# Who makes and who scales the one-hot rows when gates are spread: all eight rows in one VectorE instruction, three scaled by GpSimd

## The chip, the cores and the metric

The kernel runs on one core of one Trainium2 chip. The metric is the device time of one execution in microseconds. The compute engines of the core are TensorE (PE in the profile), VectorE (DVE), ScalarE (ACT) and GpSimd (POOL); SyncE (SP) issues transfers.

## The reference

The kernel computes one step of a small hybrid decoder: a Mamba-2 group and an RWKV-7 group, and then a mixer over 16,384 single-neuron experts ("PEER"). Only the last part bears on the change. Each token picks, for each of 8 heads, 16 experts out of 128 x 128. An expert is named by two keys, and each pick has a gate:

```python
e1 = jnp.take_along_axis(i1, pos // PEER_TOPK, axis=-1)
e2 = jnp.take_along_axis(i2, pos % PEER_TOPK, axis=-1)
experts = e1 * N_KEYS + e2
gate = jax.nn.softmax(top_s, axis=-1)
...
act = jax.nn.gelu(jnp.einsum('thkd,td->thk', ue, tb).astype(F32), approximate=False) * gate
```

So a token has 8 x 16 = 128 picks (first key, second key, gate). For 704 of the tokens the kernel doesn't gather the picked experts. It runs every expert on every token and multiplies by a dense table of gates, 128 x 128 numbers per token, which is zero where nothing was picked.

## The kernel before

The program is a row of stages: input projection, the two groups' heads, output projection, the picking of experts, the turning of some rows, `spread_gates`, and at last `run_experts`, which takes about half of the time. Each stage ends in a barrier of all engines.

`spread_gates` builds the dense table of gates. The 704 tokens are 11 groups of 64 (`GROUP_ROWS`), each group is 8 batches of 8 tokens (`BATCH`), so there are 88 batches. First TensorE turns the picks so that a token's 128 picks lie on the 128 partitions (`by_pick`: first key, second key, gate). Then, for a token t, with one partition per pick:

- `hot_i[:, t, :]` is a row of 128 numbers per pick: 1 at the first key and 0 elsewhere. VectorE makes it by comparing `iota` (0 to 127) with the key.
- `gate_j[:, t, :]` is the same for the second key, times the gate.
- TensorE multiplies the one by the other, over the picks: the result in PSUM is the token's 128 x 128 table.
- ScalarE copies eight such tables from PSUM into `spread`, and after eight batches SyncE stores that to memory.

Who makes `gate_j` is divided: for the first five tokens (`SCALED = 5`) VectorE makes only the ones, in one instruction, and ScalarE multiplies each by its gates in place (`scale`, line 2259, five instructions). For the other three VectorE makes and multiplies in one `tensor_scalar` per token (line 2302). GpSimd has no work in this stage.

`hot_i`, `gate_j`, the PSUM tables `g_ps` and `spread` have two buffers each. Batches use them in turn. Every engine runs its own program over the batches, and counting semaphores hold it: VectorE may begin batch i when the matmuls of batch i-2 are done (`g_done`); ScalarE scales when the five rows are there (`hot_ready`), and it does this for batch i+1 before it empties batch i; TensorE needs VectorE's last instruction of the batch (`batch_ready`), ScalarE's scales (`scaled`) and the emptied PSUM tables of batch i-2 (`g_out`).

Of the kernel before, what the change touches and what calls it, by code (L numbers as in the profile page):

```python
# [22 lines left out]
ALU = mybir.AluOpType  # L23
# [3 lines left out]
P = 128  # L27
# [25 lines left out]
START = 2  # L53


class Stage:
# [15 lines left out]
    def sb(self, name, shape, dt=F32):  # L72
        return self.ctx.enter_context(self.nc.sbuf_tensor(f"{self.name}_{name}", shape, dt))

    def psum(self, name, *shape):

        n = int(np.prod(shape))
        banks = self.ctx.enter_context(self.nc.psum_tensor(f"{self.name}_{name}", [P, -(-n // BANK) * BANK], F32))
        used = banks[:, 0:n]
        return used if len(shape) == 1 else used.rearrange("p (a b) -> p a b", a=shape[0])  # L80

    def sem(self, name):
        self.sems.append(self.nc.alloc_semaphore(f"{self.name}_{name}"))
        return self.sems[-1]
# [13 lines left out]
def at(dram, m):  # L98

    return dram[m] if isinstance(m, int) else dram[bass.ds(m, 1)].rearrange("a p c -> (a p) c")  # L100
# [1656 lines left out]
N_KEYS = 128  # L1757
# [417 lines left out]
BATCH = 8  # L2175

SCALED = 5


def spread_gates(nc, picks, gates_d, eye_d, iota_d):  # L2180
    with Stage(nc, "spread") as st:
        sb, psum, sem = st.sb, st.psum, st.sem
        eye, iota = sb("eye", [P, P]), sb("iota", [P, P])

        by_pick = sb("by_pick", [P, 3, ROW_GROUPS * GROUP_ROWS])
        hot_i = [sb(f"hot_i_{s}", [P, BATCH, N_KEYS]) for s in range(2)]
        gate_j = [sb(f"gate_j_{s}", [P, BATCH, N_KEYS]) for s in range(2)]
        spread = [sb(f"spread_{s}", [P, N_KEYS, GROUP_ROWS]) for s in range(2)]
        g_ps = [psum(f"g_ps_{s}", BATCH, P) for s in range(2)]
        t_ps = [psum(f"t_ps_{s}", BANK) for s in range(2)]  # L2190
        consts_loaded, turned, turned_out = sem("consts_loaded"), sem("turned"), sem("turned_out")
        batch_ready, hot_ready, scaled, g_done, g_out = sem("batch_ready"), sem("hot_ready"), sem("scaled"), sem("g_done"), sem("g_out")
        stored = [sem(f"g_stored_{s}") for s in range(2)]
        PER_GROUP = GROUP_ROWS // BATCH

        def over_groups(eng, before, batch, after):

            def group(q, s, g):
                before(q, s, g)
                with eng.Fori(0, PER_GROUP // 2) as b:  # L2200
                    for a in range(2):
                        batch(s, a, g * PER_GROUP + b * 2 + a, b * 2 + a)
                after(q, s, g)

            with eng.Fori(0, ROW_GROUPS // 2) as q:
                for s in range(2):
                    group(q, s, q * 2 + s)
            group(ROW_GROUPS // 2, 0, ROW_GROUPS - 1)

        nothing = lambda *_: None  # L2210
        with nc.Block() as block:
            @block.sync
            def _(sp):
                sp.dma_start(eye[:], eye_d).then_inc(consts_loaded, 16)
                sp.dma_start(iota[:], iota_d).then_inc(consts_loaded, 16)

                def store(q, s, g):
                    sp.wait_ge(g_out, START + g * PER_GROUP + PER_GROUP)
                    sp.dma_start(at(gates_d, g), spread[s][:].rearrange("p j t -> p (j t)")).then_inc(stored[s], 16)

                over_groups(sp, nothing, lambda *_: None, store)
                for s in range(2):
                    sp.wait_ge(stored[s], START + 16 * ((ROW_GROUPS + 1 - s) // 2))

            @block.tensor
            def _(pe):
                pe.wait_ge(consts_loaded, START + 32)
                for a, tile in enumerate(DENSE_TILES):
                    n = ROW_TILES[tile][1]
                    if a >= 2:  # L2230
                        pe.wait_ge(turned_out, START + a - 1)
                    for s in range(3):
                        mm = pe.transpose(t_ps[a % 2][:, s * P:s * P + n], picks[0:n, s, tile, :], eye[0:n, 0:n])
                    mm.then_inc(turned, 1)

                def batch(s, a, i, b):
                    pe.wait_ge(batch_ready, START + i + 1)
                    pe.wait_ge(scaled, START + i + 1)

                    pe.wait_ge(g_out, START + i - 1)  # L2240
                    for t in range(BATCH):
                        mm = pe.matmul(g_ps[a][:, t, :], hot_i[a][:, t, :], gate_j[a][:, t, :], start=True, stop=True)
                    mm.then_inc(g_done, 1)

                over_groups(pe, nothing, batch, nothing)

            @block.scalar
            def _(act):
                for a, tile in enumerate(DENSE_TILES):
                    lo, n = ROW_TILES[tile]  # L2250
                    act.wait_ge(turned, START + a + 1)
                    by_slice = t_ps[a % 2][:, 0:3 * P].rearrange("p (s t) -> p s t", s=3)[:, :, 0:n]
                    act.activation(by_pick[:, :, lo:lo + n], by_slice, ACT.Copy).then_inc(turned_out, 1)

                def scale(i, a):
                    act.wait_ge(hot_ready, START + i + 1)
                    for t in range(SCALED):
                        gate = by_pick[:, 2, bass.ds(i * BATCH + t, 1)]
                        last = act.activation(gate_j[a][:, t, :], gate_j[a][:, t, :], ACT.Copy, scale=gate)
                    last.then_inc(scaled, 1)  # L2260

                def empty(s, a, i, b):
                    act.wait_ge(g_done, START + i + 1)
                    act.activation(spread[s][:, :, bass.ds(b * BATCH, BATCH)], g_ps[a].rearrange("p t j -> p j t"), ACT.Copy).then_inc(g_out, 1)

                def group(q, s, g, pairs):
                    act.wait_ge(stored[s], START + q * 16)
                    with act.Fori(0, pairs) as b:
                        for a in range(2):
                            i = g * PER_GROUP + b * 2 + a  # L2270
                            scale(i + 1, 1 - a)
                            empty(s, a, i, b * 2 + a)


                scale(0, 0)
                with act.Fori(0, ROW_GROUPS // 2) as q:
                    for s in range(2):
                        group(q, s, q * 2 + s, PER_GROUP // 2)
                group(ROW_GROUPS // 2, 0, ROW_GROUPS - 1, PER_GROUP // 2 - 1)
                last_batch = ROW_GROUPS * PER_GROUP - 1  # L2280
                scale(last_batch, 1)
                empty(0, 0, last_batch - 1, PER_GROUP - 2)
                empty(0, 1, last_batch, PER_GROUP - 1)

            @block.vector
            def _(dve):
                dve.wait_ge(consts_loaded, START + 32)
                dve.wait_ge(turned_out, START + len(DENSE_TILES))

                def batch(s, a, i, b):  # L2290

                    dve.wait_ge(g_done, START + i - 1)
                    def hot(out, key, rows):
                        cube = [P, rows, N_KEYS]
                        return dve.tensor_tensor(out, iota[:].unsqueeze(1).broadcast_to(cube),
                                                 by_pick[:, key, bass.ds(i * BATCH, rows)].unsqueeze(2).broadcast_to(cube), ALU.is_equal)

                    hot(gate_j[a][:, 0:SCALED, :], 1, SCALED).then_inc(hot_ready, 1)
                    last = hot(hot_i[a][:], 0, BATCH)
                    for t in range(SCALED, BATCH):  # L2300
                        e2, gate = (by_pick[:, s_, bass.ds(i * BATCH + t, 1)] for s_ in (1, 2))
                        last = dve.tensor_scalar(gate_j[a][:, t, :], iota[:], e2, gate, ALU.is_equal, ALU.mult)
                    last.then_inc(batch_ready, 1)

                over_groups(dve, nothing, batch, nothing)

            @block.gpsimd
            def _(pool):
                st.start(pool)


class RowTiles:
# [664 lines left out]
```

## Time and profile before

| | |
|---|---|
| median of three runs | 4279.36 us (4277.87 to 4286.69) |
| the profiled execution: its time, its span | 4278.28 us, 4276.7 us |
| TensorE busy, share of the span | 3743.9 us, 88% |
| VectorE | 3242.4 us, 76% |
| ScalarE | 1204.4 us, 28% |
| GpSimd | 1241.3 us, 29% |
| `spread_gates`, first batch's start to last batch's copy | 1984 to 2221 us |

The shares are means over stages that differ; for a change inside one stage only that stage's rows count. In a row of the timeline or of the groups stand the line of the kernel, the engine, the operation, what it writes and reads by the program's names, and the shape as partitions x elements of one instruction. A matmul in fp32 leaves two records. An instruction's record on VectorE or ScalarE can overlap the next one's by some hundredths of a microsecond, so the pace is read from start to start.

### The profile page before, as it was taken

The numbers are of one execution on the slowest core, as the hardware profiler recorded it, in microseconds if no ns is written. First come the engines' busy times: TensorE is split into PE (matmuls) and PEld (weight loads), VectorE is DVE, ScalarE is ACT, GpSimd is POOL, SyncE is SP. The second block draws the span as 40 slices with busy tenths as digits, with TensorE's granted clock in tenths as the row PEclk, the third lists the DMA queues.
The fourth block names the chain that finished last, engine by engine and source line by source line (L and its number), as shares of the span: only waits on it lengthen the run. The fifth ranks groups of instructions, "written<-read, shape, count | busy, mean of one in ns | idle before, by whom it ended". The sixth has DMA issues, their size and how long they took to land. (4 is left out here: it accounts for less than half of the span.)

```text
span 4276.7 us, 66020 instructions
## 1 busy us (share of the span) xinstructions
PE 3743.9 (88%) x22546; PEld 3450.8 (81%) x22546; DVE 3242.4 (76%) x6415; ACT 1204.4 (28%) x2213; POOL 1241.3 (29%) x1054
## 2 busy tenths in 40 slices
PE   7998666999895868774769999999999999999997
PEld 6998554777785845443759999999999999999997
DVE  4431564666764248997977999999999999999998
ACT  3211232232322102215972222222222222222221
POOL 0211000000000000000004555556555555555563
PEclk8999566899998889887989999999999999999998
DMA  3775211000001100010458888888888888888885
GB/s 93 85 80 75 82 59 62 24 12 20 11 9 62 67 23 27 29 39 42 201 228 299 291 293 300 292 300 287 300 289 299 289 300 291 298 294 287 305 289 190
DMA packets 292099, 729.43 MB, mean 171 GB/s; under 512 B 27528, under 2 KB 138840, under 8 KB 290448
## 3 DMA queue, kind: packets, MB, share of 16 engines
q0 software_dynamic: 120560, 431.42, 32.6%
q1 hardware_dynamic: 171424, 296.57, 20.7%
q8 instruction: 60, 0.98, 0.1%
q14 instruction: 55, 0.45, 0.0%
HBM read 650.20 MB, written 77.70 MB: 170 GB/s over the span
## 5 line engine op out<-in xcount | busy, mean ns | idle before, releaser
L2512 POOL DMA_INDIRECT experts_u_row<-in_up_rows,experts_u_at x384 | 562.5, 1465 | 648.1 <-DVE experts_dot L2698 530.2
L107 PE MATMUL experts_up_ps<-experts_u_hi,experts_up_hi 128*128 128x352 f32 x2048 | 662.4, 323 | 26.8 <-DVE experts_u_lo L2674 24.7
L107 PE MATMUL experts_down_ps<-experts_act_hi,experts_down_hi 128*128 128x352 f32 x2048 | 675.4, 330 | 8.2 <-DVE experts_down_lo L2674 6.4
L108 PE MATMUL experts_down_ps<-experts_act_lo,experts_down_hi 128*128 128x352 f32 x2048 | 661.6, 323 | 0.0
L108 PE MATMUL experts_up_ps<-experts_u_lo,experts_up_hi 128*128 128x352 f32 x2048 | 661.2, 323 | 0.0
L109 PE MATMUL experts_up_ps<-experts_u_hi,experts_up_lo 128*128 128x352 f32 x2048 | 661.0, 323 | 0.0
L109 PE MATMUL experts_down_ps<-experts_act_hi,experts_down_lo 128*128 128x352 f32 x2048 | 660.9, 323 | 0.0
L2519 POOL DMA_INDIRECT experts_v_row<-in_down,experts_v_at x384 | 506.3, 1318 | 222.4 <-issue 112.8
L2698 DVE CUSTOM_DVE_ANT_0 experts_u_row<-experts_u_row,stream_u_rows_of 128x1024 f32<-128x1024 f32 x384 | 466.5, 1215 | 71.8 <-DMA experts_u_row<-in_up_rows,experts_u_at 68.8
L2711 DVE SCALAR_TENSOR_TENSOR stream_h_rows_of<-experts_v_row,experts_weight,stream_h_rows_of 128x1024 f32<-128x1024 f32 x384 | 496.0, 1292 | 14.2 <-DVE experts_weight L2703 6.8
L2717 DVE TENSOR_TENSOR stream_h<-stream_h,experts_down_ps 128x704 f32<-128x704 f32 x512 | 450.4, 880 | 68.0 <-PE experts_down_ps L109 67.1
L107 PEld LDWEIGHTS experts_down_ps<-experts_act_hi,experts_down_hi 128*128 128x128 f32 x2048 | 385.8, 188 | 31.4 <-DVE stream_h L2717 19.8
L107 PEld LDWEIGHTS experts_up_ps<-experts_u_hi,experts_up_hi 128*128 128x128 f32 x2048 | 386.2, 189 | 29.3 <-issue 21.7
L108 PEld LDWEIGHTS experts_down_ps<-experts_act_lo,experts_down_hi 128*128 128x128 f32 x2048 | 386.8, 189 | 0.0
L108 PEld LDWEIGHTS experts_up_ps<-experts_u_lo,experts_up_hi 128*128 128x128 f32 x2048 | 386.7, 189 | 0.0
L109 PEld LDWEIGHTS experts_up_ps<-experts_u_hi,experts_up_lo 128*128 128x128 f32 x2048 | 386.6, 189 | 0.0
L109 PEld LDWEIGHTS experts_down_ps<-experts_act_hi,experts_down_lo 128*128 128x128 f32 x2048 | 386.1, 189 | 0.0
L2616 ACT ACTIVATE experts_down_hi<-experts_down 128x1024 fp32r<-128x1024 f32 x128 | 135.4, 1057 | 707.6 <-PE experts_down_ps L109 707.6
L1984 PE MATMUL pick_q_ps<-picking_u,pick_w_query 128*128 128x384 f32 (+1 forms) x768 | 249.3, 485 | 44.0 <-DMA pick_sub_keys<-in_keys 44.0
L2629 ACT ACTIVATE experts_act_v<-experts_up_ps 128x352 f32<-128x352 f32 x256 | 119.0, 465 | 596.2 <-PE experts_up_ps L109 454.0
L107 PE MATMUL inp_proj<-inp_u_hi,inp_w_in_hi 128*128 128x384 f32 x648 | 222.5, 343 | 45.0 <-DVE inp_u_lo L290 23.0
L1984 PEld LDWEIGHTS pick_q_ps<-picking_u,pick_w_query 128*128 128x128 f32 x768 | 149.1, 197 | 134.7 <-issue 56.5
(380 smaller groups left out, 6626.5 us busy)
## 6 DMA issues: line engine op xcount, KB each, us to landing
experts_up<-in_up SPq DMA_DIRECT2D x128, 512.0 KB
experts_down<-in_down SPq DMA_DIRECT2D x128, 512.0 KB
gates<-spread_spread SPq DMA_DIRECT2D x11, 4096.0 KB
experts_gates<-gates SPq DMA_DIRECT2D x64, 704.0 KB
cols<-inp_done POOLq DMA_DIRECT2D x27, 576.0 KB
inp_w_in<-in_w_in SPq DMA_DIRECT2D x27, 512.0 KB
pick_w_query<-in_w_query SPq DMA_DIRECT2D x16, 512.0 KB, 4.0
experts_u_row<-in_up_rows,experts_u_at POOLq DMA_INDIRECT x384
```

The lines of the kernel that those rows point to most:

```text
L107: pe.matmul(out, w_hi, x_hi, start=start, stop=False)
L108: pe.matmul(out, w_hi, x_lo, start=False, stop=False)
L109: return pe.matmul(out, w_lo, x_hi, start=False, stop=stop)
L1984: mm = pe.matmul(q_ps[at_q % 3][:, 0:n], w[s][:, k * P:k * P + P], u[:, k, lo:lo + n], start=(k == 0), stop=(k == KD - 1))
L2512: pool.indirect_dma_start(u_row[b][:], None, up_rows_d, bass.IndirectOffsetOnAxis(ap=u_at[slot][:, b, a:a + 1], axis=0)).then_inc(u_row_lo ...
L2519: pool.indirect_dma_start(v_row[b][:], None, v_table, bass.IndirectOffsetOnAxis(ap=v_at[slot][:, b, a:a + 1], axis=0)).then_inc(v_row_load ...
L2616: act.activation(down_hi[:, e, :], down[e][:], ACT.Copy).then_inc(down_rounded, 1)
L2629: act.activation(act_v[e][:, lo:lo + n], up_ps[e][c][:, 0:n], ACT.Gelu).then_inc(gelu_ready, 1)
L2698: dve.tensor_tensor_reduce(u_row[b][:], u_row[b][:], rows.u[:, b, :], 1.0, 0.0, ALU.mult, ALU.add, dot[slot][:, b, a:a + 1]).then_inc(dott ...
L2711: dve.scalar_tensor_tensor(out=rows.h[:, b, :], in0=v_row[b][:], scalar=weight[slot][:, b, a:a + 1], in1=rows.h[:, b, :], op0=ALU.mult, op ...
L2717: dve.tensor_tensor(row, row, down_ps[m % 2][:, :, 0:DC], ALU.add).then_inc(added, 1)
```

## The change

VectorE now makes the ones of all eight second keys in one instruction, and then `hot_i`. The three `tensor_scalar` are gone. ScalarE scales rows 0 to 4 as before. GpSimd multiplies rows 5 to 7 by their gates in place, in one `tensor_tensor` per batch, when `hot_ready` is raised, and raises a new semaphore, `pool_scaled`, for which TensorE waits as well.

```diff
@@ TensorE
                     pe.wait_ge(batch_ready, START + i + 1)
                     pe.wait_ge(scaled, START + i + 1)
+                    pe.wait_ge(pool_scaled, START + i + 1)
@@ VectorE
-                    hot(gate_j[a][:, 0:SCALED, :], 1, SCALED).then_inc(hot_ready, 1)
-                    last = hot(hot_i[a][:], 0, BATCH)
-                    for t in range(SCALED, BATCH):
-                        e2, gate = (by_pick[:, s_, bass.ds(i * BATCH + t, 1)] for s_ in (1, 2))
-                        last = dve.tensor_scalar(gate_j[a][:, t, :], iota[:], e2, gate, ALU.is_equal, ALU.mult)
-                    last.then_inc(batch_ready, 1)
+                    hot(gate_j[a][:], 1, BATCH).then_inc(hot_ready, 1)
+                    hot(hot_i[a][:], 0, BATCH).then_inc(batch_ready, 1)
@@ GpSimd
+                def batch(s, a, i, b):
+                    pool.wait_ge(hot_ready, START + i + 1)
+                    rows = BATCH - SCALED
+                    cube = [P, rows, N_KEYS]
+                    pool.tensor_tensor(gate_j[a][:, SCALED:BATCH, :], gate_j[a][:, SCALED:BATCH, :],
+                                       by_pick[:, 2, bass.ds(i * BATCH + SCALED, rows)].unsqueeze(2).broadcast_to(cube), ALU.mult).then_inc(pool_scaled, 1)
+
+                over_groups(pool, nothing, batch, nothing)
```

On VectorE, inside the loop over the batches of a group, one batch read as follows before:

```order
-L2295 ISA
-L2295 TENSOR_TENSOR spread_gate_j<-spread_iota,spread_by_pick 128x640
-L2295 ISA
-L2295 TENSOR_TENSOR spread_hot_i<-spread_iota,spread_by_pick 128x1024
-L2302 ISA
-L2302 TENSOR_SCALAR spread_gate_j<-spread_iota,spread_by_pick 128x128
-L2302 ISA
-L2302 TENSOR_SCALAR spread_gate_j<-spread_iota,spread_by_pick 128x128
-L2302 ISA
-L2302 TENSOR_SCALAR spread_gate_j<-spread_iota,spread_by_pick 128x128
```

and two batches in a row read as follows after the change:

```order
+L2296 ISA
+L2296 TENSOR_TENSOR spread_gate_j<-spread_iota,spread_by_pick 128x1024
+L2296 ISA
+L2296 TENSOR_TENSOR spread_hot_i<-spread_iota,spread_by_pick 128x1024
+L2293 REGISTER_ALU
+L2296 ISA
+L2296 TENSOR_TENSOR spread_gate_j<-spread_iota,spread_by_pick 128x1024
+L2296 ISA
+L2296 TENSOR_TENSOR spread_hot_i<-spread_iota,spread_by_pick 128x1024
```

The instruction for `gate_j` grew from five rows to eight, and `hot_i` is now the last of a batch. On GpSimd, whose program went straight from the barrier ahead of the stage to the one behind it, the loop over the batches is new:

```order
+L2312 TENSOR_TENSOR spread_gate_j<-spread_gate_j,spread_by_pick 128x384
+L2309 REGISTER_ALU
+L2312 ISA
+L2312 TENSOR_TENSOR spread_gate_j<-spread_gate_j,spread_by_pick 128x384
+L2200 REGISTER_ALU
+L2200 COMPARE_AND_BRANCH
```

It has one multiply of 3 x 128 elements per partition in each batch. The programs of TensorE (but for its third wait), ScalarE and SyncE are what they were.

## Rows read from the trace of the kernel before

**Rows 1.** Windows, gate spreading: busy us of PE, PEld, DVE, ACT, POOL; granted clock; DMA, GB/s
```profile
2010.00:2220.00 210.00, 163.15 (x1279) 148.50 (x1278) 208.10 (x395) 196.07 (x475) 0.00 (x0) 1.00 0.47 200
```

**Rows 2.** Groups of the stage: busy us, mean ns | idle before, releaser
```profile
L2242 PE MATMUL spread_g_ps<-spread_gate_j,spread_hot_i 128*128 128x128 f32 x1408 | 181.8, 283 | 55.4 <-DVE spread_gate_j L2302 55.4
...
L2259 ACT ACTIVATE spread_gate_j<-spread_gate_j,spread_by_pick 128x128 f32<-128x128 f32 x440 | 138.2, 389 | 16.4 <-DVE spread_gate_j L2295 16.3
...
L2302 DVE TENSOR_SCALAR spread_gate_j<-spread_iota,spread_by_pick 128x128 f32<-128x128 f32 x264 | 74.3, 332 | 0.0
L2295 DVE TENSOR_TENSOR spread_gate_j<-spread_iota,spread_by_pick 128x640 f32<-128x640 f32 x88 | 71.2, 809 | 19.5 <-ACT spread_by_pick L2253 18.1 <-PE spread_g_ps L2242 1.4
```

**Rows 3.** Timeline in mid-stage: start, duration (us), engine, line, operation
```profile
2091.32 0.81 DVE L2295 TENSOR_TENSOR spread_gate_j<-spread_iota,spread_by_pick 128x640 f32<-128x640 f32 x1
...
2091.52 2.05 PE L2242 MATMUL spread_g_ps<-spread_gate_j,spread_hot_i 128*128 128x128 f32 x16 [0.59 <-DVE spread_gate_j L2302]
2092.05 1.21 DVE L2295 TENSOR_TENSOR spread_hot_i<-spread_iota,spread_by_pick 128x1024 f32<-128x1024 f32 x1
2092.28 1.57 ACT L2259 ACTIVATE spread_gate_j<-spread_gate_j,spread_by_pick 128x128 f32<-128x128 f32 x5 [0.16 <-DVE spread_gate_j L2295]
2093.19 0.85 DVE L2302 TENSOR_SCALAR spread_gate_j<-spread_iota,spread_by_pick 128x128 f32<-128x128 f32 x3
2093.76 1.01 ACT L2264 ACTIVATE spread_spread<-spread_g_ps 128x1024 f32 x1
2093.96 0.81 DVE L2295 TENSOR_TENSOR spread_gate_j<-spread_iota,spread_by_pick 128x640 f32<-128x640 f32 x1
...
2094.17 0.82 PE L2242 MATMUL spread_g_ps<-spread_gate_j,spread_hot_i 128*128 128x128 f32 x5 [0.60 <-DVE spread_gate_j L2302]
```

**Rows 4.** All first instructions of a batch (ns); timeline of the stage's two ends
```profile
L2295 DVE TENSOR_TENSOR spread_gate_j<-spread_iota,spread_by_pick x88: 804/808/826, 1984.2 to 2215.4; 128x640 f32<-128x640 f32 x88
...
1987.06 5.12 PE L2242 MATMUL spread_g_ps<-spread_gate_j,spread_hot_i 128*128 128x128 f32 x26 [3.93 <-DVE spread_gate_j L2302]
...
1990.97 1.02 ACT L2264 ACTIVATE spread_spread<-spread_g_ps 128x1024 f32 x1 [1.57 <-PE spread_g_ps L2242]
1991.00 0.82 DVE L2295 TENSOR_TENSOR spread_gate_j<-spread_iota,spread_by_pick 128x640 f32<-128x640 f32 x1 [1.44 <-PE spread_g_ps L2242]
...
2218.23 2.05 PE L2242 MATMUL spread_g_ps<-spread_gate_j,spread_hot_i 128*128 128x128 f32 x16 [0.59 <-DVE spread_gate_j L2302]
2220.32 1.02 ACT L2264 ACTIVATE spread_spread<-spread_g_ps 128x1024 f32<-128x1024 f32 x1 [1.61 <-PE spread_g_ps L2242]
```

**Rows 5.** Experts' stage, GpSimd's timeline: two copies beside two-input instructions of VectorE
```profile
2290.47 0.83 POOL L2500 COPY experts_u_at<-stream_expert_at 128x6 uint32<-128x6 uint32 x1
...
2307.09 0.37 POOL L2504 COPY experts_v_at<-stream_expert_at 128x6 uint32 x1
```

**Rows 6.** VectorE's timeline at those two copies
```profile
2290.37 0.89 DVE L2689 TENSOR_TENSOR experts_act_v<-experts_act_v,experts_gates 128x704 f32<-128x704 f32 x1
...
2306.20 1.21 DVE L2698 CUSTOM_DVE_ANT_0 experts_u_row<-experts_u_row,stream_u_rows_of 128x1024 f32<-128x1024 f32 x1
2307.34 0.08 DVE L2698 DVE_READ_ACCUMULATOR2_ANT experts_dot<- 128x1 f32 x1
2307.34 1.27 DVE L2711 SCALAR_TENSOR_TENSOR stream_h_rows_of<-experts_v_row,experts_weight,stream_h_rows_of 128x1024 f32<-128x1024 f32 x1
```

**Rows 7.** All copies of the two lines: ns min/median/max, first and last start
```profile
L2500 POOL COPY experts_u_at<-stream_expert_at x64: 197/807/1272, 2234.9 to 4175.7; 128x6 uint32 x60, 128x6 uint32<-128x6 uint32 x4
...
L2504 POOL COPY experts_v_at<-stream_expert_at x64: 193/369/432, 2276.9 to 4226.2; 128x6 uint32 x60, 128x6 uint32<-128x6 uint32 x4
```

**Rows 8.** GpSimd's memsets, groups by shape: busy us, mean ns
```profile
L1067 POOL MEMSET rwkv_s_seq<- 128x1024 f32 x1 | 1.0, 952 | 5.0 <-POOLq L70 5.0
...
L1068 POOL MEMSET rwkv_start_rows<- 128x128 f32 x1 | 0.2, 205 | 0.0
```

**Rows 9.** A window in an earlier stage, columns as in rows 1
```profile
990.00:1000.00 10.00, 6.91 (x56) 5.89 (x56) 9.96 (x20) 1.86 (x6) 0.00 (x0) 1.00 0.51 194
```

More of the change, by code:

```diff
@@ L2191, in spread_gates @@
         consts_loaded, turned, turned_out = sem("consts_loaded"), sem("turned"), sem("turned_out")
-        batch_ready, hot_ready, scaled, g_done, g_out = sem("batch_ready"), sem("hot_ready"), sem("scaled"), sem("g_done"), sem("g_out")
+        batch_ready, pool_scaled, hot_ready, scaled, g_done, g_out = sem("batch_ready"), sem("pool_scaled"), sem("hot_ready"), sem("scaled"), sem("g_done"), sem("g_out")
         stored = [sem(f"g_stored_{s}") for s in range(2)]
```

## The prediction

> **What bounds the kernel now.** I read the windows of the whole stage first. While the gates are spread, TensorE is busy 163 of 210 us, ScalarE 196, VectorE 208, and GpSimd not at all; the clock granted to TensorE is 1.00, its 2.4 GHz [rows 1]. So VectorE is the candidate, and the groups of the stage say the same: its instructions have next to no idle time before them once the stage runs, while the matmuls idle 55.4 us, all of it waiting for VectorE's `tensor_scalar` of line 2302 [rows 2]. Then one batch of eight tokens in the timeline [rows 3]. VectorE's first instruction of a batch starts at 2091.32 and the next batch's at 2093.96 us: the period is 2.64 us. It is made of three start-to-start steps with no gap between them: 0.73 us for the five one-hot rows of `gate_j`, 1.14 us for the eight of `hot_i` (the record says 1.21, but the next instruction starts 0.07 before its end), and 0.77 us for the three `tensor_scalar`. The others have room: ScalarE needs 1.48 + 1.00 = 2.48 us of the 2.64 and waits 0.16, TensorE needs 2.05 and waits 0.59. The first start is at 1984.2 and the last at 2215.4 [rows 4], 87 steps in 231.2 us, or 2.66 each: 87 times 2.64 is 229.7, and the missing 1.5 us are the first two batches, in which TensorE still ran at 1.2 GHz (first batch from 1987.06 to about 1990.97, 3.91 us instead of 2.05) [rows 4].
>
> The stage ends in a barrier and the next one starts behind it, so what a period gains or loses is multiplied by 88 and reaches the end undiminished. The profiled execution took 4278.28 us (span 4276.7), 1.1 us under the median of the three runs, 4279.36; the sum is made against 4278.3. About 0.2%, 8.6 us or 0.10 us per period, is what a measurement of this kernel can tell from no change.
>
> **The change part by part.** *VectorE.* Five rows become eight: the same instruction as `hot_i`'s, which the trace has at 1.14 us from start to start, in place of 0.73: +0.41. The three `tensor_scalar` go: -0.77. VectorE's own work falls from 2.64 to 2.28 us per batch. Alone, that would be 88 x 0.36 = 32 us.
>
> *The loop through two buffers.* It does not come to that, for `gate_j` of batch i+2 may only be written when the matmuls of batch i are done. Counted from the start of `gate_j` in batch i: 1.21 us to its end (five rows before: 0.81), 0.15 until ScalarE starts (2092.13 to 2092.28), 1.57 for its five scales, 0.13 until TensorE starts (as from 2094.04, VectorE's end, to 2094.17) [rows 3], 2.09 until another engine sees the batch done (2218.23 to 2220.32) and 0.03 more for VectorE (1991.00 against ScalarE's 1990.97) [rows 4]. Sum 5.18 us for two batches, 2.59 each. ScalarE's own floor is 2.48. So with a GpSimd that costs nothing the period would be 2.59 and the gain 88 x 0.05 = 4 us. The longer first instruction delays ScalarE by 0.41 us, and that eats what VectorE saves.
>
> *GpSimd's multiply.* It may start when `gate_j` is whole, 1.36 us behind its start, as ScalarE does. At that moment VectorE is already 0.22 us into `hot_i`, which has two inputs in SBUF. What happens then, the stage of before cannot show, but the experts' stage can. There GpSimd copies six words per partition, 64 times from each of two lines; the shortest copies take 0.197 and 0.193 us, the medians are 0.807 and 0.369 [rows 7]. Beside a two-input instruction of VectorE a copy takes what is left of that one: started at 2290.47 beside a plain `TENSOR_TENSOR` that ends at 2291.26, it ended at 2291.30; started at 2307.09 beside one that ends at 2307.41, at 2307.46 [rows 5, 6]. So a GpSimd instruction that reads SBUF stands still for as long as VectorE reads two tensors. The Trainium skill has this as a rule, in "SBUF — State Buffer", section "Who interferes with whom": VectorE's second input and GpSimd's read use one interface, held as an exclusive lock for a whole instruction. By that rule the two engines' times add in each batch; without it the period would be 2.59. The trace agrees where GpSimd comes second.
>
> The second copy also says who is next. VectorE had a two-input instruction ready directly behind (it starts at 2307.34, 1.27 us long), and the copy still ended at 2307.46, not at 2308.6. The waiting GpSimd instruction gets in at the boundary. That VectorE in its turn stands still for as long as GpSimd reads, no row shows (six words are over at once). I take it, since the standstill seen is complete and would be odd if it went one way only; the other answer is a rival below.
>
> So a batch becomes: `gate_j` 1.14, `hot_i` 1.14, then GpSimd's multiply while VectorE waits with the next `gate_j`. How long is a multiply of 3 x 128 elements? The trace has none. Nearest are GpSimd's memsets, 0.205 us for 128 words per partition and 0.952 for 1024 [rows 8]: 0.83 ns a word and 0.10 fixed. A multiply that ran at a memset's pace would take 0.42 us, the lower bound. One that moves its three words per element (two read, one written) one after the other: 3 x 0.32 + 0.10 = 1.06, and with 0.15 for handing over, 1.2 as the upper bound. I take two reads one after the other with the write beside them, 0.74, and 0.16 for handing over (what ScalarE needs behind VectorE): 0.90. A GpSimd that read both tensors at once is not excluded, so both ends stay in the range. The Trainium skill ("GPSIMD Engine Reference", section "Elementwise — side-by-side cycle accounting") measured 4497 ns for 2048 elements of a two-input add. Scaled to 384 that is an estimate of 0.84 us, and with it the period would be some 0.04 to 0.1 us from mine.
>
> Period 2.28 + 0.90 = 3.18 us. Nothing else is later: GpSimd ends at about 3.2, TensorE starts at 3.3 and is done at 5.4, and `gate_j` two batches on is due at 6.36; ScalarE's 2.48 and TensorE's 2.05 fit. VectorE's permit for the next `gate_j` comes at 5.4 - 3.18 = 2.2, just before `hot_i` ends, so it does ask at the boundary. Loss 3.18 - 2.64 = 0.54 us, x 87 = 47. The start is 0.5 us cheaper (the cold first batch is partly hidden), and the last batch 0.56 longer from `gate_j` to matmul: they cancel. The stores of `spread` would start every 25 instead of 21 us (eight batches), and ScalarE, which must wait for an earlier one, idles for VectorE and TensorE alone [rows 2]. GpSimd had nothing else to do here, and its next work is behind the barrier. **4278.3 + 47 = 4325 us.** With the bounds 0.42 and 1.2: GpSimd is then done at 2.8 and ScalarE's 2.93 decides when TensorE may start, but VectorE's 2.70 still sets the period: +5 us; and 3.48, +74 us. The likeliest case by itself: 4283 to 4352.
>
> **The rivals.** *GpSimd runs beside VectorE for nothing* (not slower). Period 2.59, 4274 us, inside 0.2%. It holds if the multiply, started at 1.36, is done by ScalarE's 2.93, so up to 1.57 us long; above 1.67 us it turns into a loss. For it: only six-word copies of integers show the standstill. Against: they show it each time, plain `TENSOR_TENSOR` included. 0.11. If some of my latencies of a tenth also shrink and ScalarE's 2.48 becomes the period, 88 x 0.16 = 14 us are gained, 4264: 0.04.
>
> *VectorE wins the boundary.* It then runs four instructions, 4.56 us, until it needs the first batch's matmuls; GpSimd goes 4.56 to 5.46, TensorE from 5.59, done for VectorE at 7.71. Period 3.86, +1.22 x 88 = 107, 4385 us. For it: in the row that speaks against it a one-column accumulator read (0.08 us) lies between the two instructions and may have been the gap; here there is none. 0.08.
>
> *VectorE is not held*, only GpSimd: its multiply then ends at 3.18, TensorE's batch is done for VectorE 0.13 + 2.12 later, and half of 5.43 is 2.72 per batch: +0.08 x 88 = 7, 4285 us; up to 4297 (2.85) where each slows the other somewhat. 0.08.
>
> *TensorE's clock falls.* It would be busy 2.05 of 3.18 us, 64%, with a pause of 1.1 us per batch. The trace has 1.00 beside 69% [rows 9], little above that. At 1.2 GHz a batch takes 3.91 [rows 4], and that would be the period: +1.27 x 88 = 112, 4390 us. 0.04.
>
> **How the numbers follow.** The case of 4325 has 0.65. Range 4284 to 4392: from a VectorE that is not held up to the low clock. It leaves out the cases of 4274 and 4264 and about 0.04 at its edges: 0.2 in all. Slower: 0.65 + 0.08 + 0.04, and 0.05 of the 0.08 of a VectorE not held: 0.82. Within 0.2%: 0.11 + 0.03 = 0.14. Faster: 0.04.
>
> **What would show it.** In the profile after: VectorE's `gate_j` starts about 3.18 us apart; each GpSimd multiply ends shortly behind the end of a `hot_i`, plus its own 0.8; the first instruction of a batch shows either a gap before it or more than its 1.21 us, while `hot_i` keeps 1.21; TensorE waits for GpSimd, about 1.1 us per batch, its clock 1.00; ScalarE's wait grows from 0.16 to 0.7. Starts every 2.6 us with multiplies that lie wholly inside `hot_i` would prove the lock wrong; two `gate_j` in a row, then a gap, that VectorE wins; a multiply of 1.5 us or more, that my price was off.

## The result and the profile after

The changed kernel takes 4315.47 us (median of four runs, 4311.34 to 4321.48) against 4280.38 us before in the same comparison (four runs): a ratio of 1.0081, 95% interval 1.0063 to 1.0098. It is slower by some 35 us. The profiled execution has a span of 4314.0 us. A second, later comparison (4282.72 us, six runs, against 4264.27, 17 runs) gave 1.0059 (1.0036 to 1.0082); what is known of the difference is told below.

The tile view of `gate_j` after the change gives, for each kind of instruction, its shortest, median and longest duration in ns, and the first and last start. It answers to [rows 4].

```profile
L2296 DVE TENSOR_TENSOR spread_gate_j<-spread_iota,spread_by_pick x88: 1225/1540/1850, 1997.6 to 2251.1; 128x1024 f32<-128x1024 f32 x88
L2312 POOL TENSOR_TENSOR spread_gate_j<-spread_gate_j,spread_by_pick x88: 1528/1621/1637, 1999.1 to 2252.9; 128x384 f32<-128x384 f32 x88
```

From the first to the last `gate_j` it is now 253.5 us, before 231.2: the stage lost 22.3 us, 0.26 us per batch. VectorE's comparison of 1024 elements takes 1.54 us for `gate_j`, although the same comparison for `hot_i` still takes 1.21, and GpSimd's multiply is recorded with 1.62 us. The timeline of mid-stage answers to [rows 3].

```profile
2090.41 1.62 POOL L2312 TENSOR_TENSOR spread_gate_j<-spread_gate_j,spread_by_pick 128x384 f32<-128x384 f32 x1 [1.28 <-DVE spread_gate_j L2296]
...
2091.57 1.54 DVE L2296 TENSOR_TENSOR spread_gate_j<-spread_iota,spread_by_pick 128x1024 f32<-128x1024 f32 x1 [0.23 <-PE spread_g_ps L2243]
...
2092.27 2.05 PE L2243 MATMUL spread_g_ps<-spread_gate_j,spread_hot_i 128*128 128x128 f32 x16 [0.85 <-POOL spread_gate_j L2312]
2093.03 1.21 DVE L2296 TENSOR_TENSOR spread_hot_i<-spread_iota,spread_by_pick 128x1024 f32<-128x1024 f32 x1
2093.27 1.57 ACT L2260 ACTIVATE spread_gate_j<-spread_gate_j,spread_by_pick 128x128 f32<-128x128 f32 x5 [0.42 <-DVE spread_gate_j L2296]
2093.37 1.56 POOL L2312 TENSOR_TENSOR spread_gate_j<-spread_gate_j,spread_by_pick 128x384 f32<-128x384 f32 x1 [1.34 <-DVE spread_gate_j L2296]
2094.47 1.54 DVE L2296 TENSOR_TENSOR spread_gate_j<-spread_iota,spread_by_pick 128x1024 f32<-128x1024 f32 x1 [0.23 <-PE spread_g_ps L2243]
```

`gate_j` starts at 2091.57 and 2094.47, a period of 2.90 us. VectorE doesn't start another instruction in the 0.30 us from 2091.27 (where `hot_i`, started at 2090.13, gives way after its 1.14) to 2091.57, and then its `gate_j` takes 0.32 more than 1.22. Together that is 0.62 us per batch beyond VectorE's own 2.28: 2.28 + 0.62 = 2.90. That these 0.62 us are GpSimd's is what the experiments have to show, for 0.23 of them stand here as a wait for TensorE. TensorE waits 0.85 us for GpSimd, ScalarE 0.42 for VectorE. The clock granted to TensorE stays at 1.00, its 2.4 GHz, as the windows show (columns as in [rows 1]):

```profile
2010.00:2250.00 240.00, 169.17 (x1324) 153.77 (x1323) 220.91 (x167) 204.79 (x497) 133.02 (x84) 1.00 0.41 175
```

The stage explains 22 of the 37 us by which the two spans differ. Some 13 us lie ahead of it: the first `gate_j` starts at 1997.6 instead of 1984.2. Two wide windows of the stage of the RWKV heads, first of the kernel before, then of the changed one, show most of it:

```profile
745.00:1368.00 623.00, 552.64 (x3987) 477.64 (x3986) 414.87 (x1018) 180.05 (x465) 14.65 (x24) 0.91 0.04 13
```

```profile
748.00:1382.00 634.00, 563.01 (x3984) 486.31 (x3982) 415.49 (x1018) 179.92 (x464) 14.83 (x24) 0.89 0.04 13
```

That stage runs the same instructions in both. It took 11 us longer at a mean granted clock of 0.89 instead of 0.91. Whether it belongs to the change is a question for the experiments.

### The profile page after: what moved, and what is told of

Read it like the earlier page. It is cut to its first block and busy times, and to the rows that moved or that the text cites. A ratio compares the mean times of both kernels' runs of the same rounds, so it can differ in the third digit from the quotient of the medians.

```text
span 4314.0 us, 65912 instructions
## 1 busy us (share of the span) xinstructions
PE 3756.7 (87%) x22546; PEld 3455.5 (80%) x22546; DVE 3243.1 (75%) x6151; ACT 1204.0 (28%) x2213; POOL 1428.3 (33%) x1142
## 5 line engine op out<-in xcount | busy, mean ns | idle before, releaser
L2525 POOL DMA_INDIRECT experts_v_row<-in_down,experts_v_at x384 | 556.1, 1448 | 222.8 <-issue 109.8
L2312 POOL TENSOR_TENSOR spread_gate_j<-spread_gate_j,spread_by_pick 128x384 f32<-128x384 f32 x88 | 141.7, 1610 | 644.3 <-DVE spread_gate_j L2296 644.3
```

Source lines behind the costliest of these rows:

```text
L2312: pool.tensor_tensor(gate_j[a][:, SCALED:BATCH, :], gate_j[a][:, SCALED:BATCH, :], by_pick[:, 2, bass.ds(i * BATCH + SCALED, rows)].unsque ...
L2525: pool.indirect_dma_start(v_row[b][:], None, v_table, bass.IndirectOffsetOnAxis(ap=v_at[slot][:, b, a:a + 1], axis=0)).then_inc(v_row_load ...
```

## The experiments

Two theories stood against each other. **Theory 1**: VectorE with two inputs in SBUF and a GpSimd that reads SBUF exclude each other, both ways, for as long as GpSimd's pass over its elements lasts, so that their times add. **Theory 2**: the loss is latency, as the multiply finishes late and TensorE and the loop through two buffers wait for it. The profile after fits either: its loop closes too (1.54 + 0.20 + 1.62 + 0.24 + 2.20 = 5.80 us for two batches). All measures of a stage are from the first to the last `gate_j`, 87 steps, in one profiled execution of each kernel; "per batch" is their mean, in which the slow first batches are counted, and lies a little above the period in mid-stage. The ratios are of whole executions, each to the kernel before in the same comparison. Where "one execution" stands, no interval can be given. The kernels with a side multiply on the changed kernel and the one with no multiply leave three gate rows of a batch unscaled.

| kernel | us | per batch | ratio to before, 95% |
|---|---|---|---|
| before | 231.2 | 2.66 | |
| changed | 253.5 | 2.91 | 1.0081 (1.0063 to 1.0098) |
| changed, second time | 253.5 | 2.91 | 1.0059 (1.0036 to 1.0082) |
| side multiply, three rows | 253.1 | 2.91 | 1.0058 (1.0036 to 1.0080) |
| side multiply, six rows | 307.1 | 3.53 | one execution |
| no multiply | 234.1 | 2.69 | 1.0001 (0.9985 to 1.0018) |
| row in PSUM | 234.1 | 2.69 | 1.0009 (0.9990 to 1.0027) |
| changed, four buffers for `gate_j` | 252.1 | 2.90 | 1.0052 (1.0035 to 1.0068) |
| row in PSUM, four and four | 221.4 | 2.54 | 0.9984 (0.9971 to 0.9998) |
| the same, four buffers | 198.0 | 2.28 | 0.9924 (0.9902 to 0.9947) |
| before, with side multiply | 275.1 | 3.16 | one execution |
| before, four buffers | 230.5 | 2.65 | one execution |

### A multiply that nobody waits for

```diff
                     pe.wait_ge(scaled, START + i + 1)
-                    pe.wait_ge(pool_scaled, START + i + 1)
...
-                    pool.tensor_tensor(gate_j[a][:, SCALED:BATCH, :], gate_j[a][:, SCALED:BATCH, :],
+                    pool.tensor_tensor(side_out[a][:], side_in[:],
                                        by_pick[...].unsqueeze(2).broadcast_to(cube), ALU.mult).then_inc(pool_scaled, 1)
```

> The changed kernel, but GpSimd's multiply of 3 x 128 elements per batch works on tiles of its own that nobody reads, and TensorE doesn't wait for it (the last three gate rows of a batch stay unscaled). Theory 1, VectorE's second input and GpSimd's read exclude each other both ways: the period stays 2.28 + 0.62 = 2.90 us although nobody waits for GpSimd, the stage is as long as in the changed kernel (first to last gate_j 253 us), the next gate_j is stretched or delayed by 0.6 us in all. Theory 2, the loss comes from TensorE waiting for a late multiply: the period is 2.59 us, 225 us for the stage, some 27 us less than the changed kernel.

`side_in` is filled with ones once, and GpSimd waits for its own multiply of the batch before (both left out of the diff above). The stage took 253.1 us, the period is 2.90. Its timeline:

```profile
2099.77 1.56 POOL L2316 TENSOR_TENSOR spread_side_out<-spread_side_in,spread_by_pick 128x384 f32<-128x384 f32 x1 [1.34 <-DVE spread_gate_j L2297]
...
2100.78 1.63 DVE L2297 TENSOR_TENSOR spread_gate_j<-spread_iota,spread_by_pick 128x1024 f32<-128x1024 f32 x1
...
2101.47 2.05 PE L2244 MATMUL spread_g_ps<-spread_gate_j,spread_hot_i 128*128 128x128 f32 x16 [0.85 <-ACT spread_gate_j L2261]
2102.34 1.21 DVE L2297 TENSOR_TENSOR spread_hot_i<-spread_iota,spread_by_pick 128x1024 f32<-128x1024 f32 x1
...
2103.68 1.63 DVE L2297 TENSOR_TENSOR spread_gate_j<-spread_iota,spread_by_pick 128x1024 f32<-128x1024 f32 x1
```

TensorE now waits for ScalarE, not for GpSimd, and yet nothing got faster. The whole loss is there without anybody who needs the product. Theory 2 falls here. The loop through two buffers closes in this kernel too (TensorE's start at 2101.47 is 2.21 us ahead of the next `gate_j` at 2103.68, the same last step as above), so whether the hold alone makes 2.90 is tried further below.

The same with six rows shows what the price hangs on (the side tiles grow with it).

```diff
-                    rows = 3
+                    rows = 6
```

> As the kernel with the side multiply, which nobody reads and nobody waits for, but six rows (768 elements per partition) instead of three. Theory 1 (both ways, for the whole read): GpSimd's 1.66 ns per element (0.827 us for 384, 1.039 for 512, undisturbed) add 0.64 us to the 0.62 that three rows hold, period 2.28 + 1.26 = 3.54 us, 308 us from first to last gate_j. A theory that VectorE pays a fixed price per collision and not for the length: still about 2.9, 253 us.

```profile
L2297 DVE TENSOR_TENSOR spread_gate_j<-spread_iota,spread_by_pick x88: 1225/2485/2490, 1958.6 to 2265.7; 128x1024 f32<-128x1024 f32 x88
```

307.1 us, where 308 were expected. The stretched `gate_j` of VectorE has a median of 2.485 us instead of 1.225: 1.26 us for 768 elements, 1.64 ns each, and 384 elements at that price are 0.63. VectorE pays by the number of elements that GpSimd passes over, and not a fixed price per collision. Whether it is GpSimd's reading or its writing that holds VectorE, no run separates.

This kernel also bears on TensorE's clock. A window in its stage, columns as in [rows 1]:

```profile
2000.00:2250.00 250.00, 144.37 (x1130) 131.39 (x1131) 250.00 (x141) 174.81 (x423) 156.48 (x71) 1.00 0.33 143
```

TensorE is busy 144.37 of 250 us, 58% where the forecast had 64%, and the granted clock is 1.00, its 2.4 GHz.

### The waits without the multiply

```diff
-                    pool.tensor_tensor(gate_j[a][:, SCALED:BATCH, :], gate_j[a][:, SCALED:BATCH, :],
-                                       by_pick[...].unsqueeze(2).broadcast_to(cube), ALU.mult).then_inc(pool_scaled, 1)
+                    pool.sem_inc(pool_scaled, 1)
```

> The changed kernel, but GpSimd only raises pool_scaled when hot_ready is raised and multiplies nothing (three gate rows of a batch stay unscaled). Both theories: the waits alone cost nothing, the loop through two buffers sets 2.59 us per batch, 225 to 226 us from first to last gate_j against 231.2 before and 253.5 after; gate_j back at 1.21 us. If the added waits were the cost, it would stay near 2.9.

```profile
L2296 DVE TENSOR_TENSOR spread_gate_j<-spread_iota,spread_by_pick x88: 1217/1225/1228, 1979.1 to 2213.2; 128x1024 f32<-128x1024 f32 x88
```

`gate_j` is back at 1.225 us in all 88 batches, and the stage takes 234.1 us: not 2.9 per batch, but not the 2.59 that was expected either. The timeline shows the loop:

```profile
2103.81 1.23 DVE L2296 TENSOR_TENSOR spread_gate_j<-spread_iota,spread_by_pick 128x1024 f32<-128x1024 f32 x1 [0.57 <-PE spread_g_ps L2243]
...
2105.19 1.57 ACT L2260 ACTIVATE spread_gate_j<-spread_gate_j,spread_by_pick 128x128 f32<-128x128 f32 x5 [0.39 <-DVE spread_gate_j L2296]
...
2106.95 2.05 PE L2243 MATMUL spread_g_ps<-spread_gate_j,spread_hot_i 128*128 128x128 f32 x16 [0.89 <-DVE spread_hot_i L2296]
...
2109.15 1.22 DVE L2296 TENSOR_TENSOR spread_gate_j<-spread_iota,spread_by_pick 128x1024 f32<-128x1024 f32 x1 [0.58 <-PE spread_g_ps L2243]
```

From one `gate_j` to the one two batches on: 1.38 us until ScalarE starts, 1.57 for its scales, 0.19 until TensorE starts (0.13 had been assumed), 2.20 until VectorE goes on (2.12 had been assumed). That is 5.34 us, 2.67 per batch. Note that the releaser in brackets (VectorE's `hot_i`, long done at 2106.17) is not who held TensorE at 2106.95; ScalarE, done at 2106.76, is. So VectorE's 0.36 us fewer buy nothing, even without GpSimd: the loop through two buffers takes them back. 87 times 2.67 is 232.3; the other 1.8 us lie in the first batches, where TensorE is at its lower clock (the longest matmul record of the stage has 0.577 us, the median 0.275).

### The comparison with one input in SBUF

ScalarE copies the row 0 to 127 into PSUM once, and VectorE reads it there (its wait for `iota_there` is left out of the diff):

```diff
+                act.activation(iota_ps, iota[:], ACT.Copy).then_inc(iota_there, 1)
...
-                        return dve.tensor_tensor(out, iota[:].unsqueeze(1).broadcast_to(cube),
+                        return dve.tensor_tensor(out, iota_ps.unsqueeze(1).broadcast_to(cube),
```

> The changed kernel, complete, but VectorE's comparison reads the row 0 to 127 from PSUM (ScalarE copies it there once), so that it has one input in SBUF. Theory 1 (second SBUF input of VectorE against GpSimd's read): no standstill either way, GpSimd's multiply takes 0.7 to 0.9 us from 1.4 us behind the start of gate_j, ScalarE's scales are later than it, period 2.59 us, about 225 us from first to last gate_j, 4 us less than before the change. A theory that GpSimd's multiply by itself takes 1.5 us or more: it still does, and the period is 2.6 to 2.7.

```profile
L2301 DVE TENSOR_TENSOR spread_gate_j<-spread_iota_ps,spread_by_pick x88: 1211/1225/1226, 1988.7 to 2222.8; 128x1024 f32<-128x1024 f32 x88
L2317 POOL TENSOR_TENSOR spread_gate_j<-spread_gate_j,spread_by_pick x88: 818/827/829, 1990.3 to 2224.3; 128x384 f32<-128x384 f32 x88
```

The multiply takes 0.827 us in every batch instead of 1.62, and VectorE isn't stretched. Moving 512 bytes per partition to another memory ends the standstill on both sides. Both engines still write SBUF at the same time here, and GpSimd still reads two tensors there, so it was VectorE's second input that the hold hung on. The stage takes 234.1 us, not the 225 that was expected, but the same as with no multiply at all: GpSimd's work is now free, and the loop through two buffers is what remains. Over the whole kernel nothing is gained (1.0009).

With four rows each for ScalarE and GpSimd (`SCALED = 4`) the loop gets shorter by one scale:

> As the kernel with the row in PSUM, complete, and ScalarE scales four rows of a batch, GpSimd four. Loop through two buffers 1.21 + 0.15 + 1.28 + 0.13 + 2.12 = 4.89 us, 2.44 per batch; VectorE 2.28, ScalarE 2.19. If theory 1 holds, the period is 2.44 us, 213 us from first to last gate_j, 18 us less than before the change, about 4262. If GpSimd is what stands still or is slow by itself (1.6 us or more for 3 rows, 2.1 for 4), the period is 2.7 or more.

221.4 us, 2.54 per batch. The expected 2.44 was too little by 0.1: the same two hand-overs make 0.07 of it, and the rest are the first batches, as above. GpSimd's multiply of 512 elements takes 1.039 us in this kernel: 0.212 more for 128 elements than the 0.827 for 384, 1.66 ns each, which agrees with the 1.64 that VectorE paid.

### Is it the loop or the shared read that sets 2.90?

Four buffers for `gate_j`, where VectorE waits for the matmuls of four batches before, and only its `hot_i` for those of two before (the loops then run over four batches in place of two):

```diff
-        gate_j = [sb(f"gate_j_{s}", [P, BATCH, N_KEYS]) for s in range(2)]
+        gate_j = [sb(f"gate_j_{s}", [P, BATCH, N_KEYS]) for s in range(4)]
...
-                    dve.wait_ge(g_done, START + i - 1)
+                    dve.wait_ge(g_done, START + i - 3)
...
+                    dve.wait_ge(g_done, START + i - 1)
```

> The changed kernel, complete, with four buffers for gate_j instead of two, so that VectorE may write gate_j without waiting for the matmuls of two batches before. Theory 1: the period stays 2.28 + 0.62 = 2.90 us, for the two engines' turns at SBUF alone set it; 253 us from first to last gate_j, VectorE's wait for TensorE gone and the next gate_j stretched by 0.6 instead of 0.3 us. The rival, that the loop through two buffers (1.54 + 0.20 + 1.62 + 0.24 + 2.20 = 5.80 us for two batches) sets it: the period falls to 2.5 to 2.6.

```profile
2101.52 1.84 DVE L2297 TENSOR_TENSOR spread_gate_j<-spread_iota,spread_by_pick 128x1024 f32<-128x1024 f32 x1
...
2103.28 1.21 DVE L2297 TENSOR_TENSOR spread_hot_i<-spread_iota,spread_by_pick 128x1024 f32<-128x1024 f32 x1
...
2104.42 1.84 DVE L2297 TENSOR_TENSOR spread_gate_j<-spread_iota,spread_by_pick 128x1024 f32<-128x1024 f32 x1
```

The period is still 2.90. VectorE's 0.23 us of waiting for TensorE are gone and its `gate_j` grew from 1.54 to 1.84 us: the 0.62 are now all in the record of the instruction. The loop isn't what sets 2.90, the hold is.

```profile
L2297 DVE TENSOR_TENSOR spread_gate_j<-spread_iota,spread_by_pick x88: 1226/1842/1848, 1965.5 to 2217.6; 128x1024 f32<-128x1024 f32 x88
L2314 POOL TENSOR_TENSOR spread_gate_j<-spread_gate_j,spread_by_pick x88: 1532/1626/1892, 1967.0 to 2219.6; 128x384 f32<-128x384 f32 x88
```

These rows also show who is next when both are ready. VectorE has its next `gate_j` ready when `hot_i` ends, with no wait before it, and yet of the 88 `gate_j` only the first has 1.23 us and the others 1.84 to 1.85, and no multiply is longer than 1.89. So the waiting GpSimd got in at every boundary.

The kernel before with the same four buffers is the control:

> The kernel before, complete, with four buffers for gate_j: a control for the buffers. VectorE works without a gap already, so both theories expect 2.64 us per batch and 230 to 231 us from first to last gate_j. A gain here would take from the shared read what the kernel with the row in PSUM and four buffers won.

230.5 us; buffers alone do nothing. Its one execution took 4277.64 us against 4278.91 before.

Both limits removed at once, row in PSUM, four and four, four buffers:

> Row in PSUM, ScalarE and GpSimd four rows each, four buffers for gate_j, complete. If the shared read and the loop through two buffers were the two limits, what is left is VectorE's own 2.28 us per batch (TensorE 2.05 and its wake-up 0.2, ScalarE 2.19): 199 us from first to last gate_j, 32 us less than before the change, about 0.993 of it. If something else limits, it stays at the 2.54 of the kernel with two buffers.

```profile
L2302 DVE TENSOR_TENSOR spread_gate_j<-spread_iota_ps,spread_by_pick x88: 1210/1210/1224, 1967.9 to 2165.9; 128x1024 f32<-128x1024 f32 x88
L2319 POOL TENSOR_TENSOR spread_gate_j<-spread_gate_j,spread_by_pick x88: 1030/1041/1043, 1969.4 to 2167.3; 128x512 f32<-128x512 f32 x88
```

```profile
2000.00:2150.00 150.00, 135.19 (x1066) 123.75 (x1066) 150.00 (x133) 143.13 (x333) 69.39 (x67) 1.00 0.53 228
```

198.0 us, 2.28 per batch; 4227.78 us against 4264.27 before, 0.9924 (0.9902 to 0.9947). VectorE is busy for all of the 150 us of the window. This version beats both kernels.

### What a tensor_scalar does

> The kernel before, complete, and GpSimd multiplies three rows per batch on tiles of its own that nobody reads, when hot_ready is raised. VectorE's batch is 0.73 us and 1.14 us of two-input comparisons and then 0.77 us of tensor_scalar, which has one tensor from SBUF. If only two SBUF inputs exclude GpSimd's read, the multiply's 0.62 us fall into those 0.77 and cost nothing: period 2.64 us, 231 us from first to last gate_j, tensor_scalar at 0.33 us. If a tensor_scalar in fp32 excludes GpSimd too, the period is 2.64 + 0.62 = 3.26 us, 284 us.

```profile
2101.63 1.56 POOL L2320 TENSOR_TENSOR spread_side_out<-spread_side_in,spread_by_pick 128x384 f32<-128x384 f32 x1 [1.60 <-DVE spread_gate_j L2298]
...
2102.43 0.85 DVE L2305 TENSOR_SCALAR spread_gate_j<-spread_iota,spread_by_pick 128x128 f32<-128x128 f32 x1
```

The multiply ended while VectorE was at its three `tensor_scalar`, but the first of these took 0.85 us instead of 0.33, and the period is 3.16 instead of 2.64. So not two inputs alone: this `tensor_scalar`, with one tensor from SBUF and one written there, stands still for GpSimd as well. Its two scalars per partition, the key and the gate, also lie in SBUF; whether it is they or the tensor that collides, no run separates. It was 0.52 us and not 0.62. GpSimd isn't done sooner (2103.19, which is 0.76 behind VectorE's boundary at 2102.43, as in the kernel with four buffers), so the other 0.10 lie on VectorE's side; how is open. The one execution took 4306.85 us against 4278.91. In "SBUF — State Buffer", section "Who interferes with whom", the Trainium skill counts `tensor_scalar` among the instructions that can take the shared pair, in a mode that uses both ports. The trace agrees that it waits, by those 0.52 us; in which mode it ran, no run here shows.

### The 13 us ahead of the stage

> The changed kernel once more, in five rounds. In the first comparison it took 35 us more than before, and its stage only 22 us more (first to last gate_j 253.5 against 231.2); the rest lay ahead of the stage. If what lies ahead is scatter from run to run, the ratio comes out at about 1.0052 (+22 us), as it did for the kernel with the side multiply (1.0058). If the changed program makes the earlier stages slower, it stays at 1.008 or above.

```profile
L2296 DVE TENSOR_TENSOR spread_gate_j<-spread_iota,spread_by_pick x88: 1224/1540/1847, 1949.8 to 2203.3; 128x1024 f32<-128x1024 f32 x88
```

The ratio is 1.0059, and in this execution the stage begins at 1949.8, 48 us earlier than in the first profile of the same kernel, and is as long as there to a tenth. Over the twelve profiles, which all run the same work ahead of the stage, its start scatters from 1949.8 to 1997.6. The 13 us lie well within that. In the two windows above they go with the clock granted to TensorE: the matmuls take 10.4 us more of the 11. Of the 48 us some 30 lie elsewhere, in the input projection: its last matmul starts at 422.5 in the first profile of the changed kernel, at 420.2 in the one before the change, and at 392.5 here. What decides either from one execution to the next wasn't tried. Nor is it shown why all four executions of the first comparison lie so high: the 22 us of the stage alone are a ratio of 1.0052, below its interval.

## Why the prediction was right, point by point

- *What bounds the kernel*: VectorE's 2.64 us per batch. Right: four buffers for the kernel before leave it at 2.65.
- *VectorE's own work falls to 2.28*. Right: the version without the two limits runs at 2.28.
- *The loop through two buffers takes back nearly all of it*. Right in kind. Its sum of 5.18 us was mis-sized: two hand-overs were read elsewhere. The 0.13 us are from VectorE to TensorE, and from ScalarE it is 0.19; the 2.09 in the 2.12 are from the last batch of the stage, and in mid-stage the whole term is 2.20. Measured 2.67 to 2.69 per batch instead of 2.59, so that a GpSimd that costs nothing gives no gain of 4 us but none at all (1.0001).
- *GpSimd stands still for VectorE*. Right: 1.62 us beside VectorE, 0.83 alone.
- *The waiting GpSimd gets in at the boundary*. Right, but the changed kernel doesn't show it: contrary to the forecast, VectorE's permit came about 0.23 us after `hot_i` in nearly every batch, so it was not yet ready at the boundary. The kernel with four buffers for `gate_j` shows it, at all 87 boundaries with VectorE ready. So the accumulator read in the old trace isn't needed as a gap.
- *VectorE stands still for GpSimd*. This was taken without a row. It is shown now, by 0.62 us of stretch with three rows and 1.26 with six.
- *Price of the multiply*: 0.90 us of hold were taken, with bounds of 0.42 and 1.2. It is 0.62: 384 elements at about 1.64 ns. As an instruction it takes 0.83; but what adds to VectorE's time is only the part that grows with the elements, and the fixed part (0.827 minus 0.63, 0.2 us) must lie beside VectorE's work. So the hold is shorter than "a whole instruction", as the prediction has it, and the measurement decides. That is the term that was mis-sized, by 0.28 us or 25 us of the stage's sum of 47; the stage lost 22. The 0.83 are near the prediction's estimate of 0.84, scaled from the 4497 ns for 2048 elements of the Trainium skill ("GPSIMD Engine Reference", section "Elementwise — side-by-side cycle accounting"). That estimate has 2.2 ns per element and nothing fixed, and the runs show 1.66 ns and 0.19 us fixed, so the two agree for this size and not in their parts.
- *The signs*. The one named for a wrong price, a multiply of 1.5 us or more, says nothing: the record holds the standstill as well, and by the forecast's own sum (ready at 1.36 us, held to 2.28, then 0.8) it would be 1.7. The period, the stretched first instruction and TensorE's wait for GpSimd (0.85 us, forecast 1.1) are the signs that tell.
- *The total*: 4325 was forecast, 4315 measured. That it came as near as that is luck: the first comparison carried some 13 us from ahead of the stage, of which the forecast knew nothing, in its direction. By the stage alone the step is 22 us, 0.52%, where 47 were forecast, and it is this that the second comparison (1.0059), the side multiply (1.0058) and the kernel with four buffers (1.0052) agree on.
- *TensorE's clock*. It stays at 2.4 GHz beside 70% busy (169.17 of 240 us) in the changed kernel, and beside 58% (144.37 of 250) in the one with six side rows. The forecast had 64%, as it had the period at 3.18. So the rival of a falling clock didn't come true in any of these kernels.

## What to carry to other kernels

Before work goes from VectorE to GpSimd, look at what VectorE does at that time: if its instructions read two tensors from SBUF, or are an fp32 `tensor_scalar` as here, most of GpSimd's time (0.62 of 0.83 us here) is added to VectorE's, whoever waits for the result. Only what VectorE saves beyond that is gained; here it saved 0.36 us. One small operand in PSUM lifted that. And an engine that got faster is worth only what the buffers behind it allow: here the first instruction became longer, the loop through two buffers was full, and 2.28 us per batch came only when both were repaired and the rows divided four and four.

## What the runs showed of the hardware that was not expected

- The engine that stands still shows it inside its instruction's record, not as idle time: `gate_j` 1.84 us instead of 1.22 with no wait before it (four buffers), and GpSimd's multiply 1.62 us for work of 0.83.
- The hold is shorter than the instruction that causes it: 0.62 us for a multiply of 0.83.
- A `tensor_scalar` in fp32 of 128 elements is held too, by 0.52 us.
- The twelve executions reach the start of the stage between 1949.8 and 1997.6 us, with the same work up to there.
